# A hybrid encoder step on one core: the retention streams' products with their states, queries as weights of 32 columns

## What is computed

```python
def _ret_chunk(S, qkv):
    q, k, v = qkv
    ...
    att = jnp.einsum('bhld,bhmd->bhlm', q, k) * decay
    o = (jnp.einsum('bhlm,bhme->bhle', att, v)
         + jnp.einsum('bhld,bhde->bhle', q, S) * jnp.exp(lg[:, None] * (n + 1.0))[:, :, None])
    kw = k * jnp.exp(lg[:, None] * (L - 1.0 - n))[:, :, None]
    S_new = jnp.exp(lg * L)[:, None, None] * S + jnp.einsum('bhmd,bhme->bhde', kw, v)
    return S_new, o
```

## Time and profile before

| | us |
|---|---|
| median of 3 runs | 2193.1 (2190.93 to 2193.49) |
| the profiled execution, own time | 2200.04 |
| its span in the trace | 2198.2 |
| PE busy in the span | 2140.3 |
| DVE busy | 1752.0 |
| the rounds with retention, about | 95 to 450 |
| first tile product of the mixer to its last, about | 30 to 672 |

### The profile page before, as it was taken

One profiled execution on the slowest core, in us unless ns is written; L12 is line 12 of the kernel. 1 busy time (PEld: TensorE's weight loads), 2 busy tenths in 40 slices (PEclk: granted clock), 3 DMA queues, 4 the chain that ended last, 5 costly groups with the idle time before them and its releaser, 6 DMA issues.

```text
span 2198.2 us, 31118 instructions
## 1 busy us (share of the span) xinstructions
PE 2140.3 (97%) x10569; PEld 1704.8 (78%) x10569; DVE 1752.0 (80%) x3270; ACT 624.0 (28%) x1197; POOL 856.7 (39%) x606
## 2 busy tenths in 40 slices
PE   6999999999999999999999999999998999999997
PEld 6998998999998885655565565677766888888886
DVE  2567586676675287889979989999968999999998
ACT  4212223132223111121211211233324444444434
POOL 4322122233333004575674775311154444444440
PEclk9999999999999999999999999999999999999999
DMA  5999989989893469999999999888899999999994
GB/s 196 303 318 305 306 294 333 338 296 300 299 315 118 149 201 347 327 388 412 383 411 410 372 412 413 302 284 282 281 377 414 414 414 414 414 414 413 414 414 187
DMA packets 314153, 735.42 MB, mean 335 GB/s; under 512 B 30368, under 2 KB 163232, under 8 KB 314016
## 3 DMA queue, kind: packets, MB, share of 16 engines
q1 hardware_dynamic: 189792, 439.67, 55.6%
q0 software_dynamic: 73728, 268.47, 31.1%
q10 hardware_dynamic: 50496, 25.59, 3.9%
HBM read 604.04 MB, written 129.57 MB: 334 GB/s over the span
## 4 chain that ended last, share of the span: by engine, by line
PE 37%; issue 22%; DVE 18%; DMA 10%; POOL 9%; SPq 2%; ACT 1%; DVEq 0%; POOLq 0%; ACTq 0%
PE ps L1785 7%; PE ps L1745 6%; PE ps L1843 6%; PE ps L1842 6%; PE ps L1844 6%; POOL b L703 5%; DVE b L1425 4%; POOL b L666 4%; PE ps L1800 4%; DMA b<-in_peer_v 3%; DMA b<-in_peer_v,b 3%; DMA b<-in_u_t 2%; SPq L495 2%; DMA acts<-b 1%; DVE b L1326 1%
## 5 line engine op out<-in xcount | busy, mean ns | idle before, releaser
L1785 PE MATMUL ps<-b,b 128*128 128x384 f32 x2048 | 665.6, 486 | 0.0
L703 POOL DMA_INDIRECT b<-u_rows,b x256 | 360.4, 1408 | 695.1 <-DVE b L1408 505.1
L1785 PEld LDWEIGHTS ps<-b,b 128*128 128x128 f32 x2048 | 386.8, 190 | 263.4
L666 POOL TENSOR_TENSOR b<-b,b 128x1024 fp32r<-128x1024 f32 x80 | 196.5, 2460 | 469.7 <-ACT b L716 465.8
L1425 DVE SCALAR_TENSOR_TENSOR b<-b,b,b 128x1024 f32<-128x1024 f32 x256 | 330.9, 1293 | 49.4 <-ACT b L930 24.9
L1546 PE MATMUL ps<-b,b 128*128 128x320 f32 x1152 | 363.7, 316 | 0.0
L1548 PE MATMUL ps<-b,b 128*128 128x320 f32 x1152 | 356.3, 309 | 0.0
L1547 PE MATMUL ps<-b,b 128*128 128x320 f32 x1152 | 356.2, 309 | 0.0
L1408 DVE CUSTOM_DVE_ANT_0 b<-b,b 128x1024 f32<-128x1024 f32 x256 | 312.7, 1221 | 30.3 <-DMA b<-u_rows,b 28.7
L703 POOL DMA_INDIRECT b<-in_peer_v,b x256 | 287.1, 1122 | 118.5 <-issue 76.0
L1842 PE MATMUL ps<-b,b 128*128 128x512 f32 x768 | 300.2, 391 | 11.6 <-DVE b L1472 11.6
(11 more groups left out here) (164 smaller groups left out, 2417.9 us busy)
## 6 DMA issues: line engine op xcount, KB each, us to landing
b<-in_u_t SPq DMA_DIRECT2D x256, 512.0 KB, 6.6
u_rows<-b SPq DMA_DIRECT2D x512, 128.0 KB, 4.4
b<-in_peer_v SPq DMA_DIRECT2D x128, 512.0 KB, 21.3
b<-in_w_in SPq DMA_DIRECT2D x72, 512.0 KB, 6.3
b<-in_wq SPq DMA_DIRECT2D x48, 512.0 KB, 4.4
acts<-b SPq DMA_DIRECT2D x128, 192.0 KB, 7.9
gates<-b ACTq DMA_DIRECT2D x12, 2048.0 KB, 8.2
b<-acts SPq DMA_DIRECT2D x32, 768.0 KB, 16.4
```

The source lines that it names most:

```text
L666: nc.gpsimd.tensor_tensor(lo[u][:, :], raw[:, u, :], hi[u][:, :].bitcast(F32), ALU.subtract).then_inc(lo_ready, 1)
L703: nc.gpsimd.indirect_dma_start(slots[n % SLOTS][:, :], None, u_rows if kind == "u" else v_rows, bass.IndirectOffsetOnAxis(ap=row_id[:, r_ ...
L1785: last = nc.tensor.matmul(ps[:, e % 4, 0:TD], w[:, k * P:(k + 1) * P], h2[:, k, SD:T], start=(k == 0), stop=(k == KT - 1))
```

## The change

The streams' cross products are made all at once, in step 4 before stream 0, with the roles of the operands exchanged. The scaled queries are now the weights, 32 columns of them for a pair of streams, and the states are streamed, 256 columns at a time. The pair c takes output rows 32c to 32c+31, so four column groups of the array are addressed in turn. A pair shares its rows: the queries are laid out twice, once with the odd streams' columns set to zero and once with the even streams' (the table `gq` is twice as wide), and the products of both are accumulated. The result is rows by value, [128, 256], in the upper half of bank 5. ACT copies it to SBUF in its step 5, and after stream 5 in step 6 two products with the identity turn it into banks 7 and 5, on top of the streams' own attention products, which move there from step 4. ACT's copy of these outputs in step 7 waits for this instead of the last stream's cross products.

```diff
+    own = np.stack([l // STEP % 2 == a for a in range(2)], 1)
+    gq = np.stack([np.broadcast_to(np.exp(g * (l % STEP + 1))[:, None, :] * own, (P, 2, P)) for g in lg], 1)
...
-        qg = [kv[:, 0, i * P:(i + 1) * P] for i in range(2)]
+        qg = [[kv[:, a, d * P:(d + 1) * P] for d in range(2)] for a in range(2)]
+        crow = att[:, 0:DV]
...
-                        for dst, n, w in ((dec, "dec", PROMPT), (dec_s, "dec_s", P), (gq, "gq", P)):
+                        for dst, n, w in ((dec, "dec", PROMPT), (dec_s, "dec_s", P), (gq, "gq", 2 * P)):
...
+                if t == 5:
+                    act.wait_ge(cross_done, g + 1)
+                    nc.scalar.activation(crow, ps[:, 5, DV:2 * DV], ACT.Copy).then_inc(crow_ready, 1)
                 if t == 7:
-                    act.wait_ge(cross_done, g * STREAMS + STREAMS)
+                    act.wait_ge(streams_done, g + 1)
...
-                for i in range(2):
-                    then(nc.vector.tensor_tensor(qg[i], qT[:, i, PROMPT:T], gq[:, :], ALU.mult),
-                         qg_ready, g * 2 + (i + 1))
+                for a in range(2):
+                    own = gq[:, a * P:(a + 1) * P].unsqueeze(1).broadcast_to([P, 2, P])
+                    then(nc.vector.tensor_tensor(kv[:, a, 0:DK].rearrange("p (d l) -> p d l", d=2), qT[:, :, PROMPT:T],
+                                                 own, ALU.mult), qg_ready, g * 2 + (a + 1))
...
+            def cross(g):
+                pe.wait_ge(qg_ready, g * 2 + 2)
+                for a in range(2):
+                    for c in range(STREAMS // 2):
+                        pe.wait_ge(s_loaded[2 * c + a], g * 16 + 16)
+                    for d in range(2):
+                        for c in range(STREAMS // 2):
+                            rows = slice(2 * STEP * c, 2 * STEP * (c + 1))
+                            last = nc.tensor.matmul(ps[rows, 5, DV:2 * DV], qg[a][d][:, rows], s_in[:, 2 * c + a, d, :],
+                                                    start=(a == 0 and d == 0), stop=(a == 1 and d == 1))
+                last.then_inc(cross_done, 1)
+
+            def stream_outputs(g):
+                pe.wait_ge(crow_ready, g + 1)
+                for et in range(2):
+                    cols = slice(DK + et * P, DK + (et + 1) * P)
+                    out = ps[:, 7 - 2 * et, 0:P]
+                    nc.tensor.matmul(out, kv[:, PT, cols], att[:, att_at[4]:att_at[4] + P], start=True, stop=False)
+                    last = nc.tensor.matmul(out, crow[:, et * P:(et + 1) * P], ident[:, :], start=False, stop=True)
+                last.then_inc(streams_done, 1)
+
             def stream(g, s):
-                pe.wait_ge(s_loaded[s], g * 16 + 16)
-                for et in range(2):
-                    for d in range(2):
-                        last = nc.tensor.matmul(
-                            ps[:, 7 - 2 * et, s * STEP:(s + 1) * STEP], s_in[:, s, d, et * P:(et + 1) * P],
-                            qg[d][:, s * STEP:(s + 1) * STEP], start=False, stop=(s == STREAMS - 1 and d == 1))
-                last.then_inc(cross_done, 1)
                 pe.wait_ge(kw_ready, g * 12 + (PT + s + 1))
...
-                    for et in range(2):
-                        cols = slice(DK + et * P, DK + (et + 1) * P)
-                        nc.tensor.matmul(ps[:, 7 - 2 * et, 0:P], kv[:, PT, cols], att[:, att_at[4]:att_at[4] + P],
-                                         start=True, stop=False)
-                    pe.wait_ge(qg_ready, g * 2 + 2)
+                    cross(g)
                 for s in {4: (0,), 5: (3,), 6: (5,)}.get(t, ()):
                     stream(g, s)
+                if t == 6:
+                    stream_outputs(g)
```

More of the change, by code:

```diff
@@ L164, in tables @@
     dec_s = np.stack([np.where(same, np.exp(g * np.maximum(l - m, 0)), 0.0) * scale for g in lg], 1)
-    gq = np.stack([np.broadcast_to(np.exp(g * (l % STEP + 1)), (P, P)) for g in lg], 1)
+    own = np.stack([l // STEP % 2 == a for a in range(2)], 1)
+    gq = np.stack([np.broadcast_to(np.exp(g * (l % STEP + 1))[:, None, :] * own, (P, 2, P)) for g in lg], 1)
     kcol = np.zeros((P, HEADS, PT + STREAMS))
@@ L265, in build_program @@
         dec_s = take(r, [P, P], F32)
-        gq = take(r, [P, P], F32)
+        gq = take(r, [P, 2 * P], F32)
         kcol = take(r, [P, HEADS, PT + STREAMS], F32)
@@ L408, in build_program @@
         qg_ready = sem("qg_ready")
-        cross_done = sem("cross_done")
+        cross_done = sem("cross_rows_done")
+        crow_ready = sem("cross_rows_ready")
+        streams_done = sem("streams_done")
         sq_ready = sem("sq_ready")
```

## The result

The kernel before takes 2193.98 us (median of 20 runs, 2189.19 to 2202.05), the changed one 2199.44 us (median of 20, 2193.42 to 2206.02). The ratio is 1.0023, interval 1.0014 to 1.0033: the change costs about 5.5 us. The profiled execution of the changed kernel took 2198.61 us, beside 2200.04 for the one of before. The two profiled executions stand the other way round than the medians, since single executions of one kernel scatter by some microseconds (the changed one over 12.6 us).

The account below looks back on a forecast made before the run. The chain of DVE's turns and loads was taken to bound the rounds' last part, with PE waiting. Delay of 6.35 us, clock 2.8 and 0.7 gave +9.9 us on 2193.1: 2203.0 us, range 2188 to 2213.

Parts of the forecast that it names:

- The ring: Each retention round: PE paces the first part, DVE's turns and loads the last 44 us, where PE comes early and waits.
- the end follows PE: Rival: turns are released through PE's pace, so its saving counts whole; 2189.2 us, or 2182.3 with four groups; chance 0.17.
- Delay ahead of stream 0's state product: In step 4 PE waits for states; stream 0, tile 5, stream 1, DVE's stream_state(1) and all turns wait behind it.
- The chain meets PE at one place: DVE's turns and loads depend on PE only at stream_state(1), where DVE waited 1.51 us in the second head.
- The cross products: PE, step 4: the 32 new records take 3.45 us a head, with ends of 1.7 and 6.9 us.
- only the first record of the next product can run beside it: A product's two records share a column group and follow each other, so overlap is limited: 3.45 us a head.
- four groups at once: Rival: all four column groups run together, cross products take 1.7 us; 5.5 us with the clock, 2198.6 us; chance 0.17.
- The stalls: PE waits for state loads before the cross products: 3.2, 0.2, 2.6 and 0.75 us in heads 1 to 4.
- Stream 1's delay: DVE's stream_state(1) starts later by 2.95, 1.6, 3.1 and 2.1 us in heads 1 to 4.
- How much is carried: Share of stream 1's delay reaching the end: head 1 whole, the other three by half, 6.35 us.
- The clock: Longer PE waits drop the clock at two more round starts, 2.8 us, and perhaps behind head 1's stall, 0.7 us.
- The argument from the DMA share: Head 1's engines have room (0.76), so later loads land later; head 2's are full (1.03), so the queue is more drained.

Follow-up runs that it names:

- e2: The kernel before with the streams' cross products left out and all waits for state loads kept: 2192.77 us, 0.9995.
- e1: The changed kernel with 20 constant products added on PE at the end of step 7 of every head (17.3 us together): 2201.42 us, 1.0041.
- e7: The kernel before without cross products, with 23 constant products (5.0 us) in step 4 ahead of stream 0 in every head: 2205.04 us, 1.0063.
- e11: The changed kernel with its 16 cross products ordered one column group after the other, behind the wait for all states: 2208.32 us, 1.0078.
- e5: The changed kernel with one constant product for the 16 cross products, each stream waiting for its own state before its state product: 2192.89 us, 1.0002.
- e8: The changed kernel with one DVE turn moved ahead of stream 1's state in the first three heads: 2194.98 us, 1.0011.
- e9: The kernel before with one DVE turn moved ahead of stream 1's state in the first three heads: 2190.37 us, 0.9987.
- e4: The changed kernel with one constant product for the 16 cross products, the wait for all eight states kept in step 4: 2196.15 us, 1.0020.
- e10: The kernel of e5 with 18 more constant products (15.6 us together) at the end of step 7: 2195.07 us, 1.0008.

## Why the prediction was right, and where it was off

**The ring holds.** The prediction said that PE comes early to the starts of the rounds and that what it saves there makes it wait. The waits went from 7.3 to 14.8 us; with the cross products gone altogether the time stayed (e2, 0.9995); 17.3 us more in the gaps cost about 2 (e1). The rival "the end follows PE", 2182 to 2189 us, falls with these three.

**Delay ahead of stream 0's state product is where the loss comes in.** Here the step held in kind: e7 and e11 put delay there and it reaches the end, e5 takes the wait for all states away and about 4 us go. That it acts through stream 1 and the turns fits DVE's longer waits (e7), but is argued: e8, meant to show it, gains no more than the same edit in the kernel before (e9). "The chain meets PE at one place" was too narrow; DVE waited for PE at stream 3 as well, 1.80, 2.05 and 0.82 us in the three heads before. By parts, the place of the wait costs about 4 us (e4 less e5), the cross products 1 to 2.5 us, not clear of the noise, everything else nothing measurable (e5, +0.4 with an interval from -2 to +3). The parts add up to the measured 5.5 us within these intervals.

**The cross products: mis-sized.** I took 3.45 us a head because the two records of one product share a column group and have to follow each other; measured are 1.86. That the records of one group follow each other held (0.216 us apart in e11). The step that failed is "only the first record of the next product can run beside it": the records of the other groups don't wait for it, and four start together every 0.22 us. In the order of the change four groups always have work; e11, where they don't, takes 4.50 us. So the rival "four groups at once" had the right size, and its 2198.6 us lies nearer to 2199.44 than my 2203.0. Adding it up again with its own terms gives a warning, though: it held 3.5 us for the clock.

**The stalls: right in head 1, too large behind it.** Forecast were 3.2, 0.2, 2.6 and 0.75 us, the trace shows 2.81, 0.33, 1.16 and none. Issue plus time to landing gave the first two well; in heads 3 and 4 PE came later than I had reckoned from the trace of before. These rounds began 0.6 us later, and their first 16 records took 1.7 us longer at the low clock. The sum had the low clock as a price of its own and not as something that shortens the stalls.

**Stream 1's delay.** Forecast +2.95, +1.6, +3.1, +2.1, seen +2.7, +0.3, +2.5, +2.9 in one pair of traces, 8.4 us instead of 9.75. These are marks in time, so delay of earlier heads, and of the slow start of the own round, is in the later ones; they are not four separate prices.

**How much is carried: not as I had it.** I carried head 1 whole and the rest by half, 6.35 of 9.75 us. By the medians e7 carries three quarters of 20 us and e11 all of 10.6. But in the one pair of traces head 1's 2.70 us are 0.12 at the start of the second round (184.97 against 184.85), in the very head that I carried whole; the shorter wait at stream 3 is part of why. In e11 stream 1 of head 1 is 3.0 us later still, and 2.5 of that arrive. So a first delay of this size can be swallowed and the next one not. The argument from the DMA share (room in head 1, fuller engines swallow the delay behind it) isn't borne out.

**The clock: the fall is as forecast, its price isn't shown.** All three starts fell to 0.50, and the records took 1.4 to 1.7 us longer. I put 3.5 us for it into the sum. But e2 and e5 have the same three cold starts, 3.4 and 3.7 us more of them than before, and stand at 0.9995 and 1.0002. 3.4 us is 1.0016 and 3.7 us 1.0017, above both intervals. Either it costs nothing here, or the PE work saved elsewhere in these two pays for it; e1 and e10, meant to tell, lie between the two accounts. The traces of e5 and e10 narrow it down: from the start of the round to DVE's state of stream 1 are 51.6, 53.1 and 51.1 us in e5, and 51.4, 52.8 and 49.1 in e10 with its shorter starts. In the second and third round a slow start is hardly seen there (0.2 and 0.3 us), in the fourth it is (2.0 us); each is one execution. What stays without this term is 6.35 us, near the measured 5.5, but by luck: the cross products were taken too long, the later stalls too large, and the share carried too small.

**Open.** Why a start that is 1.7 us longer isn't seen in the time where the fourth round shows it; what a wait for one state costs apart from the DMA traffic it sits in; and where the 5.5 us lie in the two profiled executions, which don't differ that way (the last product ahead of PEER, line 1566 of the kernel before, starts at about 732.9 us in both).

## What to carry to other kernels

Where an engine is busy for 97% and still waits at fixed places, look for the point at which the chain that ends last meets it: the same 4 to 5 us of PE work a head cost about 2 us in all at the end of step 7 and about 15 ahead of stream 1. When several transfers are joined into one operation, the wait moves to the last of them and everything behind it in the list; here that cost more than the operation saved. And in a list executed in order, put work whose data is ready ahead of a wait for another engine: one turn moved gave 0.9987, at least as much as taking all 26 us of cross products off PE (0.9995).

## What the hardware showed

- 32 records with 32 columns of weights and 256 streamed columns: 0.058 us each when the four column groups take turns, 0.141 on the mean in one group after another (e11), beside 0.216 for 128 columns of weights. Within one group they start 0.216 us apart, no faster than those of 128 columns. A group begins while earlier ones in the list still have records to come, beside the fifth of eight in e11. Why not sooner stays open.
- A weight load of 32 columns takes 110 ns in the median. In the changed kernel's groups of instructions over the four heads (count, min/median/max ns):

```profile
L1637 PEld LDWEIGHTS ps<-b,b x128: 106/110/177, 138.9 to 413.7; 128*32 128x32 f32 x128
```

32 loads of 110 ns are 3.5 us; in head 2 they take 1.48, so the loads too run side by side:

```profile
229.72 1.48 PEld L1637 LDWEIGHTS ps<-b,b 128*32 128x32 f32 x32 [0.70 <-issue]
```

- The length of a wait alone doesn't say whether the clock falls: behind 2.72 us it stayed, in e8 it fell behind 2.16 (0.57 on the mean of the next 3 us):

```profile
181.27 3.23 PE L1618 MATMUL ps<-b,b 128*128 128x128 f32 x16 [2.16 <-DVE b L1138]
```

- PE fell to a granted clock of 0.50 behind all waits of 4.1 us and more at the starts of the rounds, here as in e2 and e5, and behind the stall of 2.8 us in head 1 (0.72 in the mean of the next 2.6 us, then 0.50):

```profile
138.90:141.50 2.60, 2.52 (x32) 1.35 (x32) 2.50 (x4) 0.00 (x0) 0.00 (x0) 0.72 1.00 375
141.50:142.50 1.00, 1.00 (x6) 0.84 (x3) 0.97 (x2) 0.38 (x1) 0.00 (x0) 0.50 1.12 415
```
